# A hybrid attention block: the first weight tiles asked for earlier, the small vectors later

## The chip, the cores and the metric

The kernel runs on one core of one Trainium2 chip. The metric is the time of one execution on the device in microseconds (us). The engines are named as in the profile: PE (TensorE, the matrix products), PEld (its weight loads), DVE (VectorE), ACT (ScalarE), POOL (GpSimd) and SP (SyncE, which here only issues DMAs). SP, ACT and POOL each issue DMAs on a queue of their own; all queues share 16 DMA engines.

## The reference, cut to what matters

One decoder layer on 256 tokens of width 2048, in float32:

```
h    = rmsnorm(x) * norm_g                     # x: 256 x 2048
proj = h @ w_in                                # q, k, v, z of 12 + 8 heads, one forget column
                                               # for each of 8 heads, q and z of 4 heads, 3 gates
A: 12 heads, dilated windows, bias by distance from rel_bias, q and k normalised (q_norm_a, k_norm_a)
B: 8 heads, causal, bias from the running sum of log_sigmoid(forget column + b_forget)
M: 4 heads of 256 into mem;  k, v = (rmsnorm(mem) * mem_norm_g) @ w_mem_kv
u_i    = (o_i * silu(z_i)) @ w_proj_i          # i = A, B, M
merged = sum_i sigmoid(gate_i + b_gate_i) * u_i
out    = x + merged @ w_out
```

Nearly all of the time goes into the products with w_in, w_mem_kv, w_proj and w_out, whose 214 MB are each read once.

## The kernel before, in words

**Products.** Every float32 product is made of three: each operand is split into a high part of reduced precision and the rest (`hi`, `lo`), and PE adds hi*hi, hi*lo and lo*hi (L1337, L1338, L1339, in `passes`). A weight chunk of 2048 x 512 is cut into 16 k-tiles of 128 x 512. Two k-tiles make a *unit*: 2 k-tiles x 2 halves of the tokens x 3 passes = 12 matmuls of 512 columns. A load brings four k-tiles (1 MB) into one of four slots of `raw`. For each unit ACT writes `whi` (`hi`, L552), DVE subtracts and writes `wlo` (`lo`, L872), and PE multiplies (`unit`). `whi` and `wlo` have four slots, so ACT and DVE can be a few units ahead of PE. Eight units (`CU`) make a chunk, four chunks (q, k, v, z of four heads) make a *body* of 32 units; the bodies run one after the other, and after them the merge and the output projection.

**Order.** Each engine has one list of instructions, written out by hand. The work beside the products hangs on the unit number `s`: `beside_first(s)`, `beside_second(s)` and the constants `U_...` say at which unit an engine takes which extra step. In ACT's body the order at each `s` is: the turned tokens' high part (first chunk only), `hi` of unit `s`, the step of `beside_first(s)`, and then, at `s` = 10 and 11, `square` (L651): the squares of the first chunk's result for the q norm, scaled with `rsx`. `rsx` is 1/sqrt of the mean square of x: DVE adds up the mean (`msx`, at `s` = 8), Pool raises it to the power -0.5 (L509, signal `rootx`), and ACT's `square` of the first chunk waits for `rootx`.

**Start.** x is loaded in five pieces (columns 0 to 256, 256 to 512, and three of 512). PE turns them, so that the width lies on the partitions (`tokens_T`, L1429), ACT scales the turned piece with norm_g (`gx`) and writes the high part, DVE the low part. The first two pieces are turned ahead of the first product, the others at units 1, 3 and 5. Each turned pair of k-tiles raises the signal `xT` by one. `keep_clock(n)` issues n transposes whose result nobody reads (L1436). norm_g and mem_norm_g are loaded as 16 rows of 128 and turned by PE (L1441, L1442). For unit 0 the two k-tiles come as two loads of 256 KB, called tile 0 and tile 1 here.

**Pool's list.** Two memsets, nine DMAs of small vectors (six norm gains at L502, rel_bias, onehot, b_forget), then L509, then for each norm one small power. The gains are read as single words, one word or two for each partition; the source and the partition order give runs of 4 bytes. The program is built with `dynamic_dma_scratch_size=1024`.

Of the kernel before, what the change touches and what calls it, by code (L numbers as in the profile page):

```python
# [37 lines left out]
P = 128  # L38
D = 2048
S = 256  # L40
TT = S // P
KT = D // P
CW = 512
# [13 lines left out]
UK = 2  # L57
# [39 lines left out]
U_MERGEDT = 4  # L97
U_MERGED_SPLIT = (13, 14)
U_MEM_TURN = (8, 11, 14, 17)
U_MEM_SPLIT = (20, 21, 24, 25, 26, 27, 30, 31)  # L100
# [22 lines left out]
def hybrid_block(nc, x, mem, norm_g, mem_norm_g, w_in, b_forget, b_gate, rel_bias,  # L123
# [37 lines left out]

    gx_rows, gm_rows = part(0, P)[0:KT], part(P, P)[0:KT]
    x_sb = part(2 * D, 2 * D).rearrange("p (t d) -> p t d", t=TT)
# [8 lines left out]
    waste = part(3 * D, D)  # L172
    fbT = part(7936, S)[0:2 * B_HEADS]
    cT = part(7936, S)[0:B_HEADS]

# [66 lines left out]
    first_tile_in, first_half_in = [sem(f"first_tile_in{i}") for i in range(UK)], sem("first_half_in")  # L242
    g_in, mem_in = sem("g_in"), [sem(f"mem_in{i}") for i in range(2)]
    ident_in, cst_in = sem("ident_in"), sem("cst_in")
# [52 lines left out]
    with block as block:  # L297
# [3 lines left out]
        def _(sp):  # L301
# [13 lines left out]
            def loads(chunks, u0, before, beside=None):  # L315

                i = 0
                for view, col, tiles in chunks:
                    for k in range(0, tiles, LK):  # L320
                        slot = i % RING
                        if i >= RING:

                            sp.wait_ge(lo_done, u0 + 2 * (i - RING) + 2)
                        elif before is not None:
                            sp.wait_ge(lo_done, u0 + 2 * (last_use(slot, before) - before) + 2)
                        if before is None and i == 0:

                            for j in range(UK):
                                sp.dma_start(raw[:, 0, j], view[:, j, bass.ds(col, CW)]).then_inc(first_tile_in[j], 16)  # L330
                                if j == 0:
                                    sp_x(1)
                            sp.dma_start(raw[:, 0, UK:], view[:, UK:LK, bass.ds(col, CW)]).then_inc(load_in[0], 16)
                            sp_x(2)
                        elif before is None and i == 1:

                            sp.dma_start(raw[:, 1, 0:UK], view[:, k:k + UK, bass.ds(col, CW)])\
                              .then_inc(first_half_in, 16)
                            sp.dma_start(raw[:, 1, UK:], view[:, k + UK:k + LK, bass.ds(col, CW)])\
                              .then_inc(load_in[1], 16)  # L340
                            sp_x(3)
                        else:
                            load(view, col, k, slot)
                        if before is None and i == 2:
                            sp_x(4)
                        if before is None and i == 3:
                            sp.wait_ge(pre["gx"], 1)
                            mem_half(0)
                        if before is None and i == 5:
                            mem_half(1)  # L350
                            sp.dma_start(cst[:, P:], consts[:, P:]).then_inc(cst_in, 16)
                        if beside is not None:
                            beside(i)
                        i += 1
# [139 lines left out]
        def _(pool):  # L494
            pool.memset(half[:], -0.5).then_inc(pre["half"], 1)
            pool.wait_ge(pre["half"], 1)
            pool.memset(rel[32:33, :], 1.0).then_inc(pre["rel"], 1)
            with nc.allow_non_contiguous_dma(reason="vectors of a few hundred words, once"):
                for i, (g, w) in enumerate(((q_norm_a, 1), (k_norm_a, 1), (q_norm_b, 1), (k_norm_b, 1),
                                            (q_norm_m, 2), (k_norm_m, 2))):  # L500
                    col = i if w == 1 else 4 + 2 * (i - 4)
                    pool.dma_start(gains[:, col:col + w], g.rearrange("l (h p) -> p (l h)", p=P))\  # L502
                       .then_inc(small_in, 16)
            pool.dma_start(rel[0:32, :], rel_bias).then_inc(small_in, 16)
            pool.dma_start(oh[:], onehot).then_inc(small_in, 16)
            pool.dma_start(bf[:], b_forget.to_broadcast([P, B_HEADS])).then_inc(small_in, 16)
# [25 lines left out]
        def _(act):  # L532
# [23 lines left out]
            act.dma_start(x_sb[:, :, x_cols(0)], x_v[:, :, x_cols(0)]).then_inc(x_in[0], 16)  # L556
            act.dma_start(gm_rows, mem_norm_g.rearrange("l (k p) -> (l k) p", p=P)).then_inc(g_in, 16)

# [14 lines left out]
            def beside_first(s):  # L573
# [6 lines left out]
                if s in U_MEM_SQ:  # L580
# [3 lines left out]
                    for i in range(2):  # L584
                        act.wait_ge(mem_in[i], 16)
                    act.activation(waste, mem_sb[:, t], ACT.Square, accum_out=ssx[:, 2 + t:3 + t])\
                       .then_inc(pre["summ"], 1)
                if s == 1:

                    with nc.allow_non_contiguous_dma(reason="eight columns, once"):  # L590
                        act.dma_start(wf[:], w_in_v[:, :, F0:F0 + B_HEADS]).then_inc(wf_in, 16)
                if s in U_MEM_SPLIT:
                    n = U_MEM_SPLIT.index(s)
                    c = n // 2
                    act.wait_ge(pre["gx"], 1)
                    act.wait_ge(pre[f"mem_back{c}"], 16)
# [5 lines left out]
                    o.then_inc(pre["mT_hi"], 1)  # L602
                if s == 9:
                    act.wait_ge(wf_in, 16)
                    act.activation(wf_hi, wf[:], ACT.Copy).then_inc(pre["wf_hi"], 1)
                if s == 17:
                    act.wait_ge(pre["vneg"], 1)
                    act.activation(ls[3][:], ls[2][:], ACT.Exp).then_inc(pre["e"], 1)
                if s == 11:
# [3 lines left out]
                    act.dma_start(rel_dram, dvec).then_inc(pre["dvec_out"], 16)  # L613
                if s == 19:
                    act.wait_ge(pre["u"], 1)
                    act.activation(ls[5][:], ls[4][:], ACT.Ln).then_inc(pre["ln"], 1)
                if s in U_GATHER:
                    if s == U_GATHER[0]:
                        act.wait_ge(pre["dvec_out"], 16)
                    gather_bias(0, U_GATHER.index(s))  # L620
                if s == 25:
                    act.wait_ge(pre["crow_sb"], 1)
# [119 lines left out]
            def body(kind, g, b, lc, attn):  # L742

                u0 = g * BODY_U
                for s in range(BODY_U):
# [27 lines left out]
                    if kind == "ab" and s == U_BIAS:  # L773

                        act.wait_ge(turn_out, 64 * (2 * g + 2))
                        if fixed(b, 0):
                            act.wait_ge(pre["crow_out"], 16)
                            act.wait_ge(bias_out, 16 * 2)
# [82 lines left out]
        def _(dve):  # L861
# [72 lines left out]
            def logits(kind, a, step):  # L934
# [5 lines left out]
                if fixed(a, 0):  # L940
                    dve.wait_ge(bias_in, 16)
                    dve.wait_ge(pre["mT_hi"], 8)
                else:
                    dve.wait_ge(bias_in, 16 * (a - M_GROUPS) + 16)
# [138 lines left out]
            def beside_first(s):  # L1083
# [4 lines left out]
                if s == 8:  # L1088
# [6 lines left out]

                    dve.wait_ge(small_in, 16 * 9)
                    for i in range(AB_GROUPS):
# [9 lines left out]
                if s == 13:  # L1107
                    dve.wait_ge(pre["rootx"], 1)
                    dve.tensor_scalar(hrx[:], rsx[:, 0:2], 0.5, None, ALU.mult).then_inc(pre["halfx"], 1)
                if s == 9:  # L1110
                    dve.wait_ge(pre["wf_hi"], 1)
# [3 lines left out]
                if s in U_MEM_SPLIT:  # L1115
# [9 lines left out]
                    o.then_inc(pre["mT_lo"], 1)  # L1125
                if s == 14:
                    dve.wait_ge(pre["fbT"], 1)
                    dve.tensor_copy(fbT, side[0][0:2 * B_HEADS, 0:S]).then_inc(pre["fbT_sb"], 1)
                if s == 16:

# [11 lines left out]
                    dve.tensor_tensor(ls[2][:], ls[0][:], ls[1][:], ALU.min).then_inc(pre["vneg"], 1)  # L1142
                if s == 18:
                    dve.wait_ge(pre["e"], 1)
                    dve.tensor_scalar(ls[4][:], ls[3][:], 1.0, None, ALU.add).then_inc(pre["u"], 1)
                if s == 20:

# [8 lines left out]
                    dve.tensor_copy(ls[3][:], ls[7][:]).then_inc(pre["lf"], 1)  # L1156
                if s == 23:
                    dve.wait_ge(pre["ccol"], 1)
# [13 lines left out]
            def body(kind, g, attn, b=None):  # L1172
                u0 = g * BODY_U
                for s in range(BODY_U):
# [3 lines left out]
                    lo(u0, s)  # L1178
                    if s == 9 and kind == "ab":

# [36 lines left out]
            dve.wait_ge(pre["gxT"], 1)  # L1217
            dve.tensor_copy(gx[:], acc[0][1][:, 0:KT])
            dve.tensor_copy(gm[:], acc[0][1][:, KT:2 * KT]).then_inc(pre["gx"], 1)
            body("ab", 0, None, 0)  # L1220
# [111 lines left out]
        def _(pe):  # L1332
# [106 lines left out]
            keep_clock(4)  # L1439
            pe.wait_ge(g_in, 32)  # L1440
            pe.transpose(acc[0][1][:, 0:KT], gx_rows, ident[0:KT, 0:KT])  # L1441
            pe.transpose(acc[0][1][:, KT:2 * KT], gm_rows, ident[0:KT, 0:KT]).then_inc(pre["gxT"], 1)  # L1442
            keep_clock(4)
            tokens_T(0)
            keep_clock(6)
            tokens_T(1)
            keep_clock(6)

            def beside_first(s):
                if s in U_X:  # L1450
                    tokens_T(U_X.index(s))
                if s == 12:

# [8 lines left out]
                if s == 9:  # L1462

                    pe.wait_ge(pre["x_lo"], KT)
                    pe.wait_ge(small_in, 16 * 9)
                    pe.wait_ge(pre["rel"], 1)
                    pe.matmul(side[2][0:A_HEADS, 0:SEG], rel[:], oh[:], start=True, stop=True)\
                      .then_inc(pre["dvec"], 1)
                if s == 15:
                    pe.wait_ge(pre["fbT_sb"], 1)  # L1470
# [4 lines left out]
                    pe.wait_ge(pre["dvec_sb"], 1)  # L1475
                if s == 22:
                    pe.wait_ge(cst_in, 16)
# [114 lines left out]
```

## Time and profile before

| | |
|---|---|
| median of 3 runs | 1172.72 us (1172.53 to 1173.83) |
| the profiled execution's own time | 1174.71 us |
| its span, first to last instruction | 1172.9 us |
| PE busy | 1165.2 us, 99% of the span |
| DVE, ACT, POOL busy | 732.4, 546.6, 46.0 us |
| DMA | 275.85 MB, mean 235 GB/s |

The profiled execution is one run. Its span leaves out 1.8 us around the program that its own time has, and the profiled run lies 2.0 us above the median of the timed runs. So a difference is worked out inside the profile and then put on the median.

### The profile page before, as it was taken

The page shows a single profiled execution, that of the slowest core. Times are in us where ns is not written, and L with a number is a line of the kernel's source. Part 1 is how long each engine was busy: PE and PEld are TensorE (multiplying, and loading weights), DVE is VectorE, ACT ScalarE, POOL GpSimd, SP SyncE. Part 2 cuts the span into 40 slices and gives each one's busy share as a digit, 9 for nine tenths or more (in the row PEclk, how much of TensorE's full clock was granted, in tenths as well). Part 3 has the DMA queues.
Part 4 walks back from the last instruction along what each step waited for, and adds up shares of the span by engine and source line. Part 5 has one row for each costly group of instructions (what it writes and reads, how often), then busy time and mean ns, then how long its engine had stood idle before and what let it go on. Part 6 is the DMA issues. An engine that isn't in the chain of part 4 may idle for free.

```text
span 1172.9 us, 14512 instructions
## 1 busy us (share of the span) xinstructions
PE 1165.2 (99%) x5312; PEld 968.2 (83%) x5312; DVE 732.4 (62%) x905; ACT 546.6 (47%) x670; POOL 46.0 (4%) x36
## 2 busy tenths in 40 slices
PE   8999999999999999999999999999999999999998
PEld 7788888888888888888888888888888888888887
DVE  4877588576567567567566565665556556555653
ACT  4666445445445545535545444434434443443432
POOL 2111000000010000000000000000000000000000
PEclk9999999999999999999999999999999999999999
DMA  9988789658577578677677796567548546765861
GB/s 309 329 261 318 234 267 328 225 188 287 192 235 271 195 261 282 199 257 242 237 245 222 258 274 207 173 215 261 198 148 299 189 157 224 255 205 199 283 244 37
DMA packets 147613, 275.85 MB, mean 235 GB/s; under 512 B 9393, under 2 KB 32613, under 8 KB 147568
## 3 DMA queue, kind: packets, MB, share of 16 engines
q1 hardware_dynamic: 135632, 258.57, 66.0%
q10 hardware_dynamic: 11488, 16.62, 4.5%
q8 instruction: 28, 0.46, 0.2%
q0 software_dynamic: 448, 0.06, 0.1%
q14 instruction: 17, 0.14, 0.0%
HBM read 251.34 MB, written 26.24 MB: 237 GB/s over the span
## 4 chain that ended last, share of the span: by engine, by line
PE 99%; DMA 1%; SPq 0%; DVE 0%; issue 0%
PE acc L1337 32%; PE acc L1339 32%; PE acc L1338 32%; PE side L1381 1%; DMA group<-in_x_dram 1%; PE side L1373 0%; PE side L1397 0%; PE side L1406 0%; PE side L1408 0%; PE side L1404 0%; PE side L1382 0%; PE side L1429 0%; PE side L1457 0%; PE side L1459 0%; PE acc L1436 0%; PE acc L1429 0%
## 5 line engine op out<-in xcount | busy, mean ns | idle before, releaser
L872 DVE TENSOR_TENSOR w_lo<-w_raw,w_hi 128x1024 fp32r<-128x1024 f32 x407 | 496.1, 1222 | 371.5 <-ACT w_hi L552 370.8
L552 ACT ACTIVATE w_hi<-w_raw 128x1024 fp32r<-128x1024 f32 x407 | 430.0, 1060 | 540.4 <-PE acc L1339 530.7
L1337 PE MATMUL acc<-w_hi,hT_hi 128*128 128x512 f32 x1152 | 450.7, 391 | 0.1
L1338 PE MATMUL acc<-w_lo,hT_hi 128*128 128x512 f32 x1152 | 448.6, 389 | 0.0
L1339 PE MATMUL acc<-w_hi,hT_lo 128*128 128x512 f32 x1152 | 448.6, 389 | 0.0
L1337 PEld LDWEIGHTS acc<-w_hi,hT_hi 128*128 128x128 f32 x1152 | 216.6, 188 | 46.8 <-DVE w_lo L872 1.3
L1339 PEld LDWEIGHTS acc<-w_hi,hT_lo 128*128 128x128 f32 x1152 | 216.5, 188 | 45.3
L1338 PEld LDWEIGHTS acc<-w_lo,hT_hi 128*128 128x128 f32 x1152 | 216.6, 188 | 44.1
L1337 PE MATMUL acc<-w_hi,mT_hi 128*128 128x512 f32 x256 | 99.8, 390 | 0.0
L1338 PE MATMUL acc<-w_lo,mT_hi 128*128 128x512 f32 x256 | 99.6, 389 | 0.0
L1339 PE MATMUL acc<-w_hi,mT_lo 128*128 128x512 f32 x256 | 99.6, 389 | 0.0
L1339 PE MATMUL acc<-w_hi,ozT_lo 128*128 128x512 f32 x224 | 87.2, 389 | 0.0
L1337 PE MATMUL acc<-w_hi,ozT_hi 128*128 128x512 f32 x224 | 87.1, 389 | 0.0
L1338 PE MATMUL acc<-w_lo,ozT_hi 128*128 128x512 f32 x224 | 87.1, 389 | 0.0
L1337 PEld LDWEIGHTS acc<-w_hi,mT_hi 128*128 128x128 f32 x256 | 48.1, 188 | 10.2 <-issue 0.2
L1338 PEld LDWEIGHTS acc<-w_lo,mT_hi 128*128 128x128 f32 x256 | 48.1, 188 | 9.9
L1339 PEld LDWEIGHTS acc<-w_hi,mT_lo 128*128 128x128 f32 x256 | 48.1, 188 | 9.9
L1337 PEld LDWEIGHTS acc<-w_hi,ozT_hi 128*128 128x128 f32 x224 | 42.1, 188 | 8.7
L1338 PEld LDWEIGHTS acc<-w_lo,ozT_hi 128*128 128x128 f32 x224 | 42.0, 188 | 8.7
L1339 PEld LDWEIGHTS acc<-w_hi,ozT_lo 128*128 128x128 f32 x224 | 42.0, 188 | 8.7
L528 POOL TENSOR_TENSOR rs<-ms,half 128x8 f32<-128x8 f32 x8 | 20.5, 2562 | 353.4 <-DVE ms L900 353.4
L651 ACT ACTIVATE group<-acc,rsx 128x512 f32<-128x512 f32 x28 | 19.2, 686 | 21.9 <-PE acc L1339 21.2
(177 smaller groups left out, 578.6 us busy)
## 6 DMA issues: line engine op xcount, KB each, us to landing
w_raw<-in_w_in_dram SPq DMA_DIRECT2D x142, 1024.0 KB, 6.4
w_raw<-in_w_mem_kv_dram SPq DMA_DIRECT2D x16, 1024.0 KB, 6.4
w_raw<-in_w_out_dram SPq DMA_DIRECT2D x16, 1024.0 KB, 5.2
w_raw<-in_w_proj_a_dram SPq DMA_DIRECT2D x12, 1024.0 KB, 5.1
w_raw<-in_w_proj_m_dram SPq DMA_DIRECT2D x8, 1024.0 KB, 5.0
w_raw<-in_w_proj_b_dram SPq DMA_DIRECT2D x8, 1024.0 KB, 5.0
turned_oz<-group SPq DMA_DIRECT2D x44, 128.0 KB, 4.7
group<-turned_oz SPq DMA_DIRECT2D x11, 512.0 KB, 4.5
```

Source lines behind the costliest of these rows:

```text
L528: pool.tensor_tensor(rs[:], ms[:], half[:], ALU.pow).then_inc(roots, 1)
L552: act.activation(whi[:, s % RING], raw[:, slot, UK * (s % 2):UK * (s % 2) + UK], ACT.Copy)\
L651: act.activation(qn[:, t], acc[w][t][:], ACT.Square, scale=rsx[:, r:r + 1]).then_inc(squares, 1)
L872: dve.tensor_tensor(wlo[:, s % RING], raw[:, (s // 2) % RING, UK * (s % 2):UK * (s % 2) + UK], whi[:, s % RING].bitcast(F32), ALU.subtract ...
L1337: pe.matmul(banks[t][:], hi, whi[:, s % RING, j], start=first and j == 0, stop=False)
L1338: pe.matmul(banks[t][:], hi, wlo[:, s % RING, j], start=False, stop=False)
L1339: return pe.matmul(banks[t][:], lo, whi[:, s % RING, j], start=False, stop=last and j == UK - 1)
L1381: pe.matmul(side[h][:, 0:S], q2[x][:, h], k2[y][:, :, h], start=n == 0, stop=n == 2)
```

## The change

- Tile 0 is asked for on ACT's queue, right behind x's first piece, where mem_norm_g stood. On SP's queue tile 1 comes first and x's second piece after it.
- mem_norm_g is no longer loaded as rows and turned by PE with norm_g. Pool loads it straight into `gm`, in four pieces of 128 partitions x 4 single words, signal `gm_in`.
- Pool waits until six pairs of x are turned (`xT` at 6) before it asks for any small vector. rel_bias and onehot come first and have a signal of their own (`rel_in`), then the six gains, the four pieces of mem_norm_g, and b_forget.
- Four `keep_clock` transposes ahead of x's first piece go; behind the first piece there are nine for six, behind the second two for six.
- The forget column's weights (wf) are asked for at unit 4 instead of 1, and the steps that hang on them come three units later on every engine. DVE's step with the gains moves from unit 8 to 12, and its copy of the gain from unit 9 to 13.
- The tiles fbT and cT move within `group`; DVE's first logits wait for `crow_out` instead of ACT's load of the bias.

```diff
+U_GAINS = 12
-    gx_rows, gm_rows = part(0, P)[0:KT], part(P, P)[0:KT]
+    gx_rows = part(0, P)[0:KT]
-    fbT = part(7936, S)[0:2 * B_HEADS]
-    cT = part(7936, S)[0:B_HEADS]
+    fbT = part(6144, S)[0:2 * B_HEADS]
+    cT = part(6144 + S, S)[0:B_HEADS]
...
-                            for j in range(UK):
-                                sp.dma_start(raw[:, 0, j], view[:, j, bass.ds(col, CW)]).then_inc(first_tile_in[j], 16)
-                                if j == 0:
-                                    sp_x(1)
+                            sp.dma_start(raw[:, 0, 1], view[:, 1, bass.ds(col, CW)]).then_inc(first_tile_in[1], 16)
+                            sp_x(1)
...
             pool.memset(rel[32:33, :], 1.0).then_inc(pre["rel"], 1)
+            pool.wait_ge(pre["xT"], 6)
+            pool.dma_start(rel[0:32, :], rel_bias).then_inc(rel_in, 16)
+            pool.dma_start(oh[:], onehot).then_inc(rel_in, 16)
...
                     pool.dma_start(gains[:, col:col + w], g.rearrange("l (h p) -> p (l h)", p=P))\
                        .then_inc(small_in, 16)
-            pool.dma_start(rel[0:32, :], rel_bias).then_inc(small_in, 16)
-            pool.dma_start(oh[:], onehot).then_inc(small_in, 16)
+                for k in range(0, KT, 4):
+                    pool.dma_start(gm[:, k:k + 4], mem_norm_g.rearrange("l (k p) -> p (l k)", p=P)[:, k:k + 4])\
+                       .then_inc(gm_in, 16)
             pool.dma_start(bf[:], b_forget.to_broadcast([P, B_HEADS])).then_inc(small_in, 16)
             pool.wait_ge(pre["rel"], 1)
             pool.wait_ge(pre["meanx"], 1)
...
-            act.dma_start(gm_rows, mem_norm_g.rearrange("l (k p) -> (l k) p", p=P)).then_inc(g_in, 16)
+            view, col = body_chunks("a", 0)[0]
+            act.dma_start(raw[:, 0, 0], view[:, 0, col:col + CW]).then_inc(first_tile_in[0], 16)
-                if s == 1:
+                if s == 4:
                         act.dma_start(wf[:], w_in_v[:, :, F0:F0 + B_HEADS]).then_inc(wf_in, 16)
-                    act.wait_ge(pre["gx"], 1)
+                    act.wait_ge(gm_in, 64)
                     act.wait_ge(pre[f"mem_back{c}"], 16)
...
-                            act.wait_ge(pre["crow_out"], 16)
...
+                    dve.wait_ge(pre["crow_out"], 16)
...
-                    dve.wait_ge(small_in, 16 * 9)
+                if s == U_GAINS:
+                    dve.wait_ge(small_in, 16 * 7)
...
-                    if s == 9 and kind == "ab":
+                    if s == (U_GAINS + 1 if fixed(g, 0) else 9) and kind == "ab":
...
-            dve.tensor_copy(gm[:], acc[0][1][:, KT:2 * KT]).then_inc(pre["gx"], 1)
+            dve.tensor_copy(gx[:], acc[0][1][:, 0:KT]).then_inc(pre["gx"], 1)
...
             keep_clock(4)
-            pe.wait_ge(g_in, 32)
-            pe.transpose(acc[0][1][:, 0:KT], gx_rows, ident[0:KT, 0:KT])
-            pe.transpose(acc[0][1][:, KT:2 * KT], gm_rows, ident[0:KT, 0:KT]).then_inc(pre["gxT"], 1)
-            keep_clock(4)
+            pe.wait_ge(g_in, 16)
+            pe.transpose(acc[0][1][:, 0:KT], gx_rows, ident[0:KT, 0:KT]).then_inc(pre["gxT"], 1)
             tokens_T(0)
-            keep_clock(6)
+            keep_clock(9)
             tokens_T(1)
-            keep_clock(6)
+            keep_clock(2)
...
-                    pe.wait_ge(small_in, 16 * 9)
+                    pe.wait_ge(rel_in, 16 * 2)
```

The steps on the forget column that come three units later are not repeated here: on PE 12 to 15, 15 to 18 and 22 to 25; on DVE 9 to 12, 14 to 17, 16 to 19, 18 to 21, 20 to 23 and 23 to 26; on ACT 9 to 12, 17 to 20, 19 to 22 and 25 to 28.

## Rows read from the trace of the kernel before

**Rows 1.** The page: busy time by engine, and the chain's shares by engine.
```profile
PE 1165.2 (99%) x5312; PEld 968.2 (83%) x5312; DVE 732.4 (62%) x905; ACT 546.6 (47%) x670; POOL 46.0 (4%) x36
...
PE 99%; DMA 1%; SPq 0%; DVE 0%; issue 0%
```

**Rows 2.** The timeline of the start: us, duration, instruction, idle time before it.
```profile
2.13 0.45 SPq L313 DMA_DIRECT2D group<-in_x_dram  x1
2.62 0.47 SPq L330 DMA_DIRECT2D w_raw<-in_w_in_dram  x1
...
8.70 1.11 PE L1429 MATMUL side<-cst,group 128*128 128x128 f32 x4 [0.83 <-DMA group<-in_x_dram]
9.21 0.63 ACT L541 ACTIVATE w_hi<-w_raw 128x512 fp32r<-128x512 f32 x1 [1.17 <-DMA w_raw<-in_w_in_dram]
...
9.60 1.49 PE L1436 MATMUL acc<-cst 128*128 128x128 f32 x6
...
10.74 0.78 PE L1337 MATMUL acc<-w_hi,hT_hi 128*128 128x512 f32 x1
...
12.17 0.63 PE L1337 MATMUL acc<-w_hi,hT_hi 128*128 128x512 f32 x1
...
12.60 0.50 PE L1338 MATMUL acc<-w_lo,hT_hi 128*128 128x512 f32 x1
...
12.93 0.39 PE L1339 MATMUL acc<-w_hi,hT_lo 128*128 128x512 f32 x1
...
13.16 0.39 PE L1337 MATMUL acc<-w_hi,hT_hi 128*128 128x512 f32 x1
```

**Rows 3.** DMA issues: line, count, KB each, us from issue to landing.
```profile
wf<-in_w_in_dram ACTq DMA_DIRECT2D x1, 64.0 KB, 18.9
mem_means<-msx POOLq DMA_DIRECT2D x4, 0.2 KB, 7.6
...
group<-in_norm_g_dram SPq DMA_DIRECT2D x1, 8.0 KB, 2.3
...
gains<-in_q_norm_a_dram POOLq DMA_DIRECT2D x1, 0.5 KB, 4.3
...
gains<-in_q_norm_m_dram POOLq DMA_DIRECT2D x1, 1.0 KB, 7.9
gains<-in_k_norm_m_dram POOLq DMA_DIRECT2D x1, 1.0 KB, 5.2
```

**Rows 4.** The timeline of Pool alone, to the first power.
```profile
1.33 0.74 POOL L502 DMA_DIRECT2D gains<-in_q_norm_a_dram  x1 [0.33 <-issue]
...
3.14 0.56 POOL L502 DMA_DIRECT2D gains<-in_k_norm_b_dram  x1
3.67 0.76 POOL L502 DMA_DIRECT2D gains<-in_q_norm_m_dram  x1
11.91 0.74 POOL L502 DMA_DIRECT2D gains<-in_k_norm_m_dram  x1 [7.49 <-issue]
...
13.72 0.57 POOL L506 DMA_DIRECT2D bf<-in_b_forget_dram  x1
36.05 0.74 POOL L509 TENSOR_TENSOR rsx<-msx,half 128x2 f32<-128x2 f32 x1 [21.76 <-DVE msx L1093]
```

**Rows 5.** The timeline of ACT alone, around its first squares.
```profile
37.41 0.69 ACT L651 ACTIVATE group<-acc,rsx 128x512 f32<-128x512 f32 x1 [1.15 <-PE acc L1339]
38.00 1.05 ACT L552 ACTIVATE w_hi<-w_raw 128x1024 fp32r<-128x1024 f32 x1
...
42.64 1.05 ACT L552 ACTIVATE w_hi<-w_raw 128x1024 fp32r<-128x1024 f32 x1
```

**Rows 6.** The timeline of PE alone: the turned x at unit 3, unit 11's first product.
```profile
21.18 1.04 PE L1429 MATMUL acc<-cst,group 128*128 128x128 f32 x8
...
46.34 0.39 PE L1337 MATMUL acc<-w_hi,hT_hi 128*128 128x512 f32 x1
```

**Rows 7.** The page's costliest groups: busy us, mean ns of one, idle before.
```profile
L872 DVE TENSOR_TENSOR w_lo<-w_raw,w_hi 128x1024 fp32r<-128x1024 f32 x407 | 496.1, 1222 | 371.5 <-ACT w_hi L552 370.8
```

More of the change, by code:

```diff
@@ L242, in hybrid_block @@
     first_tile_in, first_half_in = [sem(f"first_tile_in{i}") for i in range(UK)], sem("first_half_in")
-    g_in, mem_in = sem("g_in"), [sem(f"mem_in{i}") for i in range(2)]
+    g_in, gm_in, rel_in, mem_in = sem("g_in"), sem("gm_in"), sem("rel_in"), [sem(f"mem_in{i}") for i in range(2)]
     ident_in, cst_in = sem("ident_in"), sem("cst_in")
@@ L602, in beside_first @@
                     o.then_inc(pre["mT_hi"], 1)
-                if s == 9:
+                if s == 12:
                     act.wait_ge(wf_in, 16)
                     act.activation(wf_hi, wf[:], ACT.Copy).then_inc(pre["wf_hi"], 1)
-                if s == 17:
+                if s == 20:
                     act.wait_ge(pre["vneg"], 1)
@@ L613, in beside_first @@
                     act.dma_start(rel_dram, dvec).then_inc(pre["dvec_out"], 16)
-                if s == 19:
+                if s == 22:
                     act.wait_ge(pre["u"], 1)
@@ L620, in beside_first @@
                     gather_bias(0, U_GATHER.index(s))
-                if s == 25:
+                if s == 28:
                     act.wait_ge(pre["crow_sb"], 1)
@@ L1109, in beside_first @@
                     dve.tensor_scalar(hrx[:], rsx[:, 0:2], 0.5, None, ALU.mult).then_inc(pre["halfx"], 1)
-                if s == 9:
+                if s == 12:
                     dve.wait_ge(pre["wf_hi"], 1)
@@ L1125, in beside_first @@
                     o.then_inc(pre["mT_lo"], 1)
-                if s == 14:
+                if s == 17:
                     dve.wait_ge(pre["fbT"], 1)
                     dve.tensor_copy(fbT, side[0][0:2 * B_HEADS, 0:S]).then_inc(pre["fbT_sb"], 1)
-                if s == 16:
+                if s == 19:
                     dve.wait_ge(pre["fb"], 1)
@@ L1142, in beside_first @@
                     dve.tensor_tensor(ls[2][:], ls[0][:], ls[1][:], ALU.min).then_inc(pre["vneg"], 1)
-                if s == 18:
+                if s == 21:
                     dve.wait_ge(pre["e"], 1)
                     dve.tensor_scalar(ls[4][:], ls[3][:], 1.0, None, ALU.add).then_inc(pre["u"], 1)
-                if s == 20:
+                if s == 23:
                     dve.wait_ge(pre["ln"], 1)
@@ L1156, in beside_first @@
                     dve.tensor_copy(ls[3][:], ls[7][:]).then_inc(pre["lf"], 1)
-                if s == 23:
+                if s == 26:
                     dve.wait_ge(pre["ccol"], 1)
@@ L1217, in _ @@
             dve.wait_ge(pre["gxT"], 1)
-            dve.tensor_copy(gx[:], acc[0][1][:, 0:KT])
-            dve.tensor_copy(gm[:], acc[0][1][:, KT:2 * KT]).then_inc(pre["gx"], 1)
+            dve.tensor_copy(gx[:], acc[0][1][:, 0:KT]).then_inc(pre["gx"], 1)
             body("ab", 0, None, 0)
@@ L1451, in beside_first @@
                     tokens_T(U_X.index(s))
-                if s == 12:
+                if s == 15:
                     pe.wait_ge(pre["x_lo"], KT)
@@ L1468, in beside_first @@
                       .then_inc(pre["dvec"], 1)
-                if s == 15:
+                if s == 18:
                     pe.wait_ge(pre["fbT_sb"], 1)
@@ L1475, in beside_first @@
                     pe.wait_ge(pre["dvec_sb"], 1)
-                if s == 22:
+                if s == 25:
                     pe.wait_ge(cst_in, 16)
```

## The prediction

> **What bounds the kernel now.** I read the page first, then the timeline of the first 50 us engine by engine, then the landings of the DMAs, and last who waits for whom. The page shows one limit: PE is busy for 1165.2 of 1172.9 us, and the chain that ended last is 99% PE [rows 1]. So a moment in which PE has no product to start is lost for good, since nothing later has slack in which to win it back; and work on ACT, DVE or Pool costs something only if PE ends up waiting for it. The reader is to see two places. The first is the start: PE waits for x's second piece until 8.70, turns it, spends 1.49 us on six dummy transposes, and starts its first product at 10.74; products come 0.43 us apart until 12.9 and 0.23 us apart after that, as 512 columns do at 1.2 and at 2.4 GHz [rows 2]. The second is unit 11, whose first product starts at 46.34 [rows 6]: PE has run without a gap up to there, and what has to be ready for it passes through ACT, which at 37.41 takes the first square (L651) with a factor that Pool worked out at 36.05 (L509) [rows 4, 5]. Today Pool's queue is empty by then: its last DMA was issued at 13.72, and it stood idle for 21.76 us before that small operation [rows 4].
>
> **The change part by part. The start.** Tile 0 of the weights moves to ACT's queue in place of mem_norm_g, tile 1 moves ahead of x's second piece, and Pool's nine DMAs leave the start. Tile 1 and the x piece then trade places: today the x piece sets PE going at 8.70 and tile 1 sets ACT going at 9.21, with issues 0.49 us apart [rows 2]. I take the x piece at 8.7 as before, because one transfer more is ahead of it and the small ones are gone; the bounds are half a microsecond earlier and one later. Behind its transposes two dummies stand in place of six. At 1.49 us for six, that is some 0.9 us with the overlap of their ends, so the first product starts near 9.9. If the spacing still falls at 12.9, two products more are done by then, worth 0.23 us each: **0.4 us gained**. The transposition of mem_norm_g and the other dummies that go or come ahead of the x piece cost nothing, because PE waits for that piece; without that wait (0.83 us) nine dummies for six would cost 0.6. Bounds: 0.9 us gained if the faster spacing comes as much earlier, 0.3 us lost if the x piece comes one microsecond later. The three units by which the forget-gate steps and wf move cost nothing: they hang on wf, which took 18.9 us to land [rows 3]; asked for at unit 4, near 23, it lands near 42 for a step that ACT reaches behind its w_hi of unit 12, which starts at 42.64 [rows 5]. The wait for crow_out moves from ACT at unit 28 to DVE a body later, behind everything it waits for. If these covers were gone, each would cost the part of its own wait that exceeds PE's lead of one to two units (2.7 us each).
>
> **Pool's queue.** This is the part that I expect to decide. All of Pool's DMAs now stand behind a wait for the sixth turned pair of x, and four new ones join them: mem_norm_g in pieces of 128 x 4 single words. Behind all of them in Pool's order stands L509, and ACT waits for that. So I follow Pool's clock.
>
> The eight transposes that hold the sixth pair start at 21.18 and take 1.04 us [rows 6]; 0.4 us earlier, Pool starts at 21.8. A DMA of Pool takes it 0.56 us for 128 single words and 0.76 us for 256 [rows 4]. rel, oh and four vectors take 6 x 0.56 = 3.34 us, so q_norm_m is issued at 25.14.
>
> Now the sixth vector. In the trace Pool issued five (4 x 128 and 256 words: 768) and then stood still for 7.49 us, to 11.91, with "issue" as the only reason [rows 4]. The fifth had been issued at 3.67 and took 7.9 us to land, which is 11.57 [rows 3, 4]: Pool went on 0.34 us after the landing. I read this as a limit on single words in flight, at least 768 and below the 1,024 that the sixth would have made. Two pieces of mem_norm_g are 1,024 words, so by the same rows no two of them can be in flight: the second, third and fourth each wait for the one before to land. And rel, oh and the first five vectors make some 833 pieces (32 and 33 rows, and 768 words), so that k_norm_m waits for q_norm_m as it does now. That is four waits for a landing. 
> One landing, from issue: 5.2 us for 256 words among running loads (k_norm_m), 7.9 us for 256 words behind four others (q_norm_m), 7.6 us for mem_means, and 4.3 us at the least (q_norm_a) [rows 3]. I take 6.0 for all four, nearest to k_norm_m because the loads run then too, and more than it because 512 words are twice as many. No row has 512 single words; the bounds are 4.3 and 7.9.
>
> So k_norm_m is issued at 25.14 + 6.0 + 0.34 = 31.48, the first piece at 32.22, the second at 38.56, the third at 44.90, the fourth at 51.24. The fourth takes 1.16 us to issue (0.20 more for each 128 words), b_forget 0.57: **Pool is free at 53.0**, or 28.97 + 4 landings. Then L509 0.74, ACT's square 0.59 to the next instruction, the w_hi behind it 1.05 [rows 4, 5], its w_lo 1.22 [rows 7] and 0.1 of handing on: unit 11 starts at 56.7. Without the wait it would start at 46.34 - 0.4 = 45.94. **PE stands still for 10.8 us.**
>
> Behind ACT's stopped square are queued w_hi of unit 11 and all later ones, two squares of mem and the rel copy; DVE's w_lo waits for ACT, and PE for DVE. DVE's own wait for the vectors at unit 12 ends with b_forget's landing near 58 and comes no later than its turn.
>
> **After the stall.** PE idled before 8.70 and then its products came 0.43 us apart until it had been busy to 12.9, 4.2 us on [rows 2]. If that recurs, some ten products cost 0.20 us more each: **2.0 us**, and they cover the squares that ACT catches up on meanwhile. Bounds: nothing if the clock stays at 2.4 GHz and ACT keeps up, 3.6 us if both cost.
>
> **The sum**, on the profiled execution: span 1172.9 - 0.4 + 10.8 + 2.0 = 1185.3 us, 12.4 more. Its own time was 1174.71 (1.8 around the span) and the median of the three runs 1172.72, so the median should be **1185.1 us**.
>
> **Rivals.** *Single words are slower still.* The five landings (from 1.33 + 4.3 to 3.67 + 7.9) show the last one 2.5 us behind the fourth. If 512 words take 2.5 us more than k_norm_m's 256, each piece takes 7.7, and q_norm_m 7.9 as before: Pool is free at 60.0, PE stands for 17.8 us, and the time is near 1192. The longer landing of mem_means speaks for it, k_norm_m's 5.2 against.
>
> *Landings are short, and nothing is lost.* This ends on the other side. PE isn't stopped if Pool is free by 42.2, that is, if the four landings take 3.3 us each or less. norm_g on SP's queue landed in 2.3 [rows 3]; with that Pool is free at 38.2, unit 11 isn't held, and only the 0.4 us remain: 1172.3. Against it, all the DMAs of Pool shown took 4.3 us and more. The Trainium skill (DMA: Bandwidth & Descriptors, Anatomy of one DMA — SWDGE (gpsimd) path) has about 2.0 us and the bytes at 436 GB/s for a DMA from Pool, which is this rival; the trace's 5.2 us for 1 KB is against it here.
>
> *The limit is one of five DMAs, not of words, or there is none.* Five at a time makes two waits: the fifth is issued at 24.0 and lands at 30.0, the tenth at 33.6 and 39.6, and the last three are out near 43. Unit 11 then starts at 46.7, 0.8 late, and the time is 1173.1. With no limit Pool is through at 32 and the time is 1172.3. The halt after exactly five allows the count as well; the trace holds no case that parts it from the words.
>
> **How the numbers follow.** The stall by four landings near 6 us: 0.66. The slower words: 0.19. Short landings: 0.05. A limit by count or none: 0.09. A start that gains over 0.2% (2.3 us, about what a measurement of this kernel can tell from no change): 0.01, because all products before 12.9 at double speed give less. So slower 0.85, same 0.14, faster 0.01. Landings of 4.3 us give a stall of 4.0 us and, with no loss after it, 1176.3; landings of 7.9 with the larger loss after it give 1194.3. The range is 1177 to 1194; it leaves out the 0.14 at 1172 to 1173 and a little above.
>
> **What would show it.** Right: Pool's timeline has four halts after q_norm_m and between the pieces of mem_norm_g, L509 starts near 53, ACT's first square is put down to Pool, and PE has one gap of 9 to 18 us before unit 11. The start shows the first product near 9.9. Wrong: L509 stays near 36, or it comes late and ACT's square does not wait; or the halts are there but each is under 3.3 us. A further gap of PE at units 15 to 25 would mean that the moved forget-gate steps are not covered.

## The result and the profile after

The changed kernel takes 1180.99 us (median of 4 executions, 1180.44 to 1181.64) against 1173.24 for the one before: 7.75 us more, ratio 1.0064 with a 95% interval of 1.0052 to 1.0076. It is slower, as forecast, by 62% of the 12.4 us that were forecast, and inside the range.

The page after: busy time by engine, the chain's shares, and one of the costliest groups (busy, mean ns | idle before, releaser). They answer to [rows 1, 7].

```profile
PE 1164.5 (99%) x5306; PEld 966.9 (82%) x5306; DVE 732.0 (62%) x904; ACT 545.6 (46%) x670; POOL 48.0 (4%) x40
...
PE 97%; issue 2%; POOL 1%; DMA 0%; DVE 0%; ACT 0%; POOLq 0%; ACTq 0%
...
L1341 PE MATMUL acc<-w_hi,hT_hi 128*128 128x512 f32 x1152 | 451.4, 392 | 7.4 <-DVE w_lo L875 7.4
```

PE is as busy as before; what is new is Pool in the chain, and one idle stretch of 7.4 us ahead of a product that waited for DVE's `w_lo`. It is the only gap of PE behind the start. Pool's timeline after shows where it comes from; it answers to [rows 4].

```profile
18.96 0.71 POOL L498 DMA_DIRECT2D rel<-in_rel_bias_dram  x1 [17.97 <-PE acc L1433]
...
22.36 0.74 POOL L504 DMA_DIRECT2D gains<-in_q_norm_m_dram  x1
28.73 0.74 POOL L504 DMA_DIRECT2D gains<-in_k_norm_m_dram  x1 [5.63 <-issue]
29.46 0.77 POOL L507 DMA_DIRECT2D gm<-in_mem_norm_g_dram  x1
35.65 0.76 POOL L507 DMA_DIRECT2D gm<-in_mem_norm_g_dram  x1 [5.42 <-issue]
41.40 0.75 POOL L507 DMA_DIRECT2D gm<-in_mem_norm_g_dram  x1 [5.00 <-issue]
45.13 0.76 POOL L507 DMA_DIRECT2D gm<-in_mem_norm_g_dram  x1 [2.98 <-issue]
45.87 0.55 POOL L509 DMA_DIRECT2D bf<-in_b_forget_dram  x1
46.55 0.72 POOL L512 TENSOR_TENSOR rsx<-msx,half 128x2 f32<-128x2 f32 x1
```

Seven DMAs go out in a row, then Pool halts four times with "issue" as the only reason, at the four places that were forecast. Its power (L509 before, L512 here) starts at 46.55 in place of 36.05. ACT's timeline follows, with one line of DVE's; it answers to [rows 5].

```profile
47.37 0.69 ACT L655 ACTIVATE group<-acc,rsx 128x512 f32<-128x512 f32 x1 [14.87 <-POOL rsx L512]
47.95 1.05 ACT L555 ACTIVATE w_hi<-w_raw 128x1024 fp32r<-128x1024 f32 x1
48.90 1.90 ACT L590 ACTIVATE group<-group 128x2048 f32<-128x2048 f32 x1
...
52.55 1.05 ACT L555 ACTIVATE w_hi<-w_raw 128x1024 fp32r<-128x1024 f32 x1
...
54.02 1.22 DVE L875 TENSOR_TENSOR w_lo<-w_raw,w_hi 128x1024 fp32r<-128x1024 f32 x1
```

ACT stands for 14.87 us and names Pool. The `w_hi` at 47.95 is unit 11's, the one at 52.55 unit 12's; between them lie the square of mem, the rel copy and the second square that had queued up. DVE's line is unit 12's `w_lo`, which ends at 55.24. PE's timeline, which answers to [rows 2, 6]:

```profile
7.52 0.60 PE L1433 MATMUL side<-cst,group 128*128 128x128 f32 x4
...
8.09 0.48 PE L1341 MATMUL acc<-w_hi,hT_hi 128*128 128x512 f32 x1
...
42.56 0.39 PE L1343 MATMUL acc<-w_hi,hT_lo 128*128 128x512 f32 x1
50.31 0.80 PE L1341 MATMUL acc<-w_hi,hT_hi 128*128 128x512 f32 x1 [7.36 <-DVE w_lo L875]
50.90 0.63 PE L1342 MATMUL acc<-w_lo,hT_hi 128*128 128x512 f32 x1
51.33 0.63 PE L1343 MATMUL acc<-w_hi,hT_lo 128*128 128x512 f32 x1
...
55.31 0.48 PE L1341 MATMUL acc<-w_hi,hT_hi 128*128 128x512 f32 x1
```

x's second piece is turned at 7.52 and the first product starts at 8.09, in place of 8.70 and 10.74. The last product of unit 10 starts at 42.56, so unit 11 was due some 0.23 us later, at 42.8. From the power's start at 46.55 to unit 11 at 50.31 it is 3.76 us. Unit 11 then lasts to 55.31, 5.0 us in place of 2.7, with most of its products 0.43 us apart. The stretches around it, in a view of busy time by engine with the granted clock (third column from the right) and DMA share and GB/s:

```profile
30.00:43.00 13.00, 12.95 (x55) 9.60 (x53) 5.74 (x10) 2.50 (x3) 1.73 (x3) 1.00 1.07 358
43.00:50.00 7.00, 0.00 (x0) 0.00 (x0) 0.97 (x1) 2.63 (x3) 2.01 (x3) 0.87 0.12 12
50.00:55.00 5.00, 4.69 (x11) 3.73 (x12) 3.75 (x6) 4.29 (x6) 0.81 (x1) 0.50 0.50 118
```

In the gap PE does nothing, and the loads stop too (12 GB/s): SP waits 15.5 us for DVE's turning of mem (L1083), which stands behind the same `w_lo` in DVE's list. The granted clock is at half in the stretch after it, the 1.2 GHz level.

### The profile page after: what moved, and what is told of

Read it like the earlier page. It is cut to its first block, busy times and chain, and to the rows that moved or that the text cites. A ratio compares the mean times of both kernels' runs of the same rounds, so it can differ in the third digit from the quotient of the medians.

```text
span 1179.2 us, 14504 instructions
## 1 busy us (share of the span) xinstructions
PE 1164.5 (99%) x5306; PEld 966.9 (82%) x5306; DVE 732.0 (62%) x904; ACT 545.6 (46%) x670; POOL 48.0 (4%) x40
## 4 chain that ended last, share of the span: by engine, by line
PE 97%; issue 2%; POOL 1%; DMA 0%; DVE 0%; ACT 0%; POOLq 0%; ACTq 0%
PE acc L1341 31%; PE acc L1343 31%; PE acc L1342 31%; PE side L1385 1%; PE side L1377 0%; PE side L1401 0%; PE side L1410 0%; PE side L1412 0%; PE side L1408 0%; PE side L1386 0%; POOL gains L504 0%; DMA cst<-in_consts_dram 0%; PE acc L1440 0%; POOL gm L507 0%; PE side L1433 0%
```

## The experiments

The theory: thirteen DMAs stand ahead of Pool's power, and the room for their single words makes Pool halt for landings. The main rivals: the moved forget-gate steps cost the time; the single words cost by their presence, wherever they stand; the limit is a count of DMAs. Medians of before beside these runs were 1172.9 to 1173.2.

**Pool's part alone.** The kernel before, with only Pool's list (and what reads it) from the change; tiles, dummies and steps as before.

```diff
+            pool.wait_ge(pre["xT"], 6)
+            pool.dma_start(rel[0:32, :], rel_bias).then_inc(rel_in, 16)
+            pool.dma_start(oh[:], onehot).then_inc(rel_in, 16)
...
+                for k in range(0, KT, 4):
+                    pool.dma_start(gm[:, k:k + 4], mem_norm_g.rearrange("l (k p) -> p (l k)", p=P)[:, k:k + 4])\
+                       .then_inc(gm_in, 16)
```

> The kernel before with Pool's part of the change alone: Pool waits for the sixth turned pair of x, then asks for rel_bias, onehot, the gains, mem_norm_g in four pieces and b_forget, all ahead of its first power; the order of the first tiles, the dummies and the forget-gate steps are those of the kernel before. If Pool's order alone is the loss, PE stands still ahead of unit 11 for 6 to 8 us and the time is 1180 to 1182. If the loss needs the earlier start, which brings ACT to its square sooner, the gap is shorter by as much: 1178 to 1180. If other parts cause it: 1173.

1181.99 us, ratio 1.0069 (1.0053 to 1.0084). The timelines of Pool, ACT and PE, one line each:

```profile
47.56 0.72 POOL L514 TENSOR_TENSOR rsx<-msx,half 128x2 f32<-128x2 f32 x1
48.37 0.69 ACT L655 ACTIVATE group<-acc,rsx 128x512 f32<-128x512 f32 x1 [14.34 <-POOL rsx L514]
51.31 0.79 PE L1341 MATMUL acc<-w_hi,hT_hi 128*128 128x512 f32 x1 [7.04 <-DVE w_lo L875]
```

The power is late, ACT names Pool, and PE stands for 7.0 us ahead of unit 11. The other parts are not needed for the loss.

**The same DMAs behind the power.** The changed kernel, mem_norm_g's pieces moved behind the first norm's power.

```diff
                 pool.tensor_tensor(rs[:, 0:n], ms[:, 0:n], half[:, 0:n], ALU.pow).then_inc(roots, 1)
+                if i == 0:
...
+                        for k in range(0, KT, 4):
+                            pool.dma_start(gm[:, k:k + 4], mem_norm_g.rearrange("l (k p) -> p (l k)", p=P)[:, k:k + 4])\
+                               .then_inc(gm_in, 16)
```

> The changed kernel with the four pieces of mem_norm_g still on Pool, but asked for behind the power and behind the first norm's power. The same DMAs with the same halts, now with nothing behind them that anyone waits for. If it is the place in Pool's order that costs, the power starts near 32.5, three halts of 3 to 6 us show up later, PE has no gap, 1169.5 to 1170.5 us. If these single-word DMAs cost by their presence (contention with the loads), part of the loss stays: 1173 or more. If the moved steps are the cause: 1179 to 1181.

1172.48 us, ratio 1.0000 (0.9990 to 1.0010): 8.5 us less than the changed kernel. Pool's timeline:

```profile
33.88 0.72 POOL L509 TENSOR_TENSOR rsx<-msx,half 128x2 f32<-128x2 f32 x1 [2.51 <-DVE msx L1099]
44.39 2.54 POOL L513 TENSOR_TENSOR rs<-ms,half 128x8 f32<-128x8 f32 x1 [9.79 <-DVE ms L905]
46.90 0.81 POOL L517 DMA_DIRECT2D gm<-in_mem_norm_g_dram  x1
53.24 0.76 POOL L517 DMA_DIRECT2D gm<-in_mem_norm_g_dram  x1 [5.54 <-issue]
```

The power waits for DVE again, the halts are still there, and PE has no gap. So it is the place in Pool's order, not the words or the moved steps. The time did not fall to the 1170 that was expected; the second profile of the kernel before, below, says why.

**Twice the room.** The changed kernel with one number changed.

```diff
-    nc = _bacc.Bacc("TRN2", ..., dynamic_dma_scratch_size=1024)
+    nc = _bacc.Bacc("TRN2", ..., dynamic_dma_scratch_size=2048)
```

> The changed kernel with one number changed: 2048 bytes reserved for Pool's descriptors in place of 1024. If the halts come from the room for descriptors, nine DMAs go out without a halt, the second piece of mem_norm_g waits for the vectors to land near 28, at most one more halt follows, Pool is free by 30 to 34, PE is not stopped, 1169.5 to 1171 us. If they come from a count of DMAs, or from each such DMA waiting for the one before it whatever the room, the four halts stay and so does the time, 1180 to 1181.

1173.15 us, ratio 1.0001 (0.9991 to 1.0011). Pool's timeline:

```profile
25.03 0.77 POOL L507 DMA_DIRECT2D gm<-in_mem_norm_g_dram  x1
30.26 1.50 POOL L507 DMA_DIRECT2D gm<-in_mem_norm_g_dram  x2 [4.46 <-issue]
36.93 0.75 POOL L507 DMA_DIRECT2D gm<-in_mem_norm_g_dram  x1 [5.17 <-issue]
37.67 0.55 POOL L509 DMA_DIRECT2D bf<-in_b_forget_dram  x1
38.35 0.72 POOL L512 TENSOR_TENSOR rsx<-msx,half 128x2 f32<-128x2 f32 x1
```

Nine DMAs go out before the first halt, and there are two halts in place of four. The room sets the halts, then, not a fixed count and not each DMA by itself. The power still starts at 38.35, later than the 30 to 34 expected, and ACT waits 5.4 us for Pool; PE waits only 0.2 us, ahead of unit 12. As with the last kernel, the time did not come down to what was expected, 1169.5 to 1171 here.

**The kernel before once more**, for a second profile.

> The kernel before, unchanged, for a second profile. The profiled execution of before took 1174.7 us and its granted clock rose to 2.4 GHz at 12.8 us; the timed ones took 1172.3 to 1173.9. If the moment of the rise varies from execution to execution, this one rises near 10 to 11, its first products come 0.23 us apart sooner, its span is near 1171, and most of the 3.5 us that the changed kernel was ahead at unit 8 was the difference between two executions and no gain of the change. If the rise stays at 12.8 and the span near 1172.9, the gain of the start was real and something later in the mended kernel gives it back.

1172.57 us, span 1170.8. PE's timeline:

```profile
7.56 0.66 PE L1429 MATMUL side<-cst,group 128*128 128x128 f32 x4 [0.20 <-DMA group<-in_x_dram]
8.06 0.82 PE L1436 MATMUL acc<-cst 128*128 128x128 f32 x6
8.63 0.48 PE L1337 MATMUL acc<-w_hi,hT_hi 128*128 128x512 f32 x1
8.95 0.39 PE L1338 MATMUL acc<-w_lo,hT_hi 128*128 128x512 f32 x1
...
12.16 1.09 PE L1429 MATMUL side<-cst,group 128*128 128x128 f32 x8 [0.53 <-DMA group<-in_x_dram]
13.34 0.50 PE L1337 MATMUL acc<-w_hi,hT_hi 128*128 128x512 f32 x1
```

The same program has its first product at 8.63, not 10.74, at 0.23 us spacing from the start; unit 8 starts at 35.0 in place of 37.2. The trace's record of the full clock begins at 6.7 us here and at 12.8 in the execution of [rows 2], some 6 us later; x's second piece, too, is turned at 7.56 and not at 8.70. Of the 3.5 us that the changed kernel was ahead at unit 8 (33.7), 2.2 were the difference between two executions of the same program. The other 1.3 are not shown to be a gain: the kernel with the pieces behind the power has the changed kernel's start and begins unit 8 at 35.05.

**The start alone**: the kernel before with the new order of tiles and dummies; the vectors at the start, the steps where they were, mem_norm_g's pieces behind the first norm's power.

```diff
+                            sp.dma_start(raw[:, 0, 1], view[:, 1, bass.ds(col, CW)]).then_inc(first_tile_in[1], 16)
+                            sp_x(1)
...
-            keep_clock(6)
+            keep_clock(9)
             tokens_T(1)
-            keep_clock(6)
+            keep_clock(2)
```

> The kernel before with the order of the first tiles and the numbers of dummies of the changed one, and with mem_norm_g on Pool behind the first norm's power; vectors at the start, steps where they were. If the start is what the change gains by, 1172.3 to 1172.7, some 0.4 us under the kernel before; if the gain needed the vectors out of the way, 1173.

1173.89 us, ratio 1.0003 (0.9994 to 1.0012): no gain from the order. PE's timeline shows why:

```profile
12.40 1.09 PE L1434 MATMUL side<-cst,group 128*128 128x128 f32 x8 [1.03 <-DMA group<-in_x_dram]
```

The first product starts at 8.37, 0.26 us sooner than in the second profile of the kernel before. But x's third piece, which unit 1 needs, lands no sooner: PE waits 1.03 us for it in place of 0.53, and turns it at 12.40 in place of 12.16. With the vectors behind it, PE turns it in the changed kernel at 10.95, without a wait.

**The steps back**: the kernel with the pieces behind the power, with wf and the forget-gate steps at their old units. It differs from the one just told by Pool's wait for x alone.

```diff
-                if s == 4:
+                if s == 1:
                         act.dma_start(wf[:], w_in_v[:, :, F0:F0 + B_HEADS]).then_inc(wf_in, 16)
...
```

> The mended kernel (mem_norm_g's pieces behind the first norm's power) with wf and the forget-gate steps back at the units of the kernel before. If moving them by three units costs nothing, the time stays at 1172.5 (1171.9 to 1173.1). If the moved steps took from what the start gives, this one is 1 to 2 us faster than 1172.5; if they give something, it is slower.

1172.47 us against 1172.48 with the steps moved: moving them costs and gives nothing that can be measured. Against the start alone it is 1.4 us less, though the two intervals (0.9983 to 1.0001 here) overlap a little; the last pair below shows it more clearly. What the change gains at all comes from the vectors that wait.

**The vectors at the start, Pool's wait for x removed** from the changed kernel.

```diff
-            pool.wait_ge(pre["xT"], 6)
```

> The changed kernel without Pool's wait for the sixth turned pair of x, so that its thirteen DMAs start near 1 us. The halts stay, four of about 5 us, and Pool is free near 29, ahead of the mean: no gap of PE. But the single words are back among the first transfers. If they were what made x's second piece late, the first product comes later than 8.1 and the time lies between 1170 and 1173; if the order of the tiles alone made the start faster, the first product stays near 8.1 and the time is 1169.5 to 1170.5. If the loss comes from the moved steps: 1179 to 1181.

1174.26 us, ratio 1.0015 (1.0005 to 1.0024), outside every range expected. The halts were 5.3 to 7.1 us, longer than expected, so Pool's power started at 34.98, not 29. The first product came at 8.9. The waits of ACT, DVE and PE:

```profile
36.17 0.69 ACT L654 ACTIVATE group<-acc,rsx 128x512 f32<-128x512 f32 x1 [1.23 <-POOL rsx L511]
44.62 1.30 DVE L1082 STREAM_TRANSPOSE group<-group 128x512 f32<-128x512 f32 x2 [5.55 <-DMA turned_mem<-group]
48.41 0.50 PE L1340 MATMUL acc<-w_hi,hT_hi 128*128 128x512 f32 x1 [1.96 <-DVE w_lo L874]
```

ACT waits 1.2 us for Pool, and unit 11 starts at 43.57 without a wait: the stall goes when Pool starts early enough, as the theory has it. PE's gap of 2.0 us comes later, ahead of unit 12, and is not Pool's power. Unit 12's `w_hi` was done at 42.4; its `w_lo` came late because DVE had first waited 5.55 us for the transfer of mem's turned rows out to memory. Why that transfer took so long here is not shown, and the profiled execution lies 1.6 us above the median, so the gap need not be in every one.

**mem_norm_g from ACT's queue**, in one DMA behind wf.

```diff
+                        act.dma_start(gm[:], mem_norm_g.rearrange("l (k p) -> p (l k)", p=P)).then_inc(gm_in, 16)
```

> The changed kernel with the four pieces of mem_norm_g taken off Pool and loaded in one DMA from ACT's queue at unit 4. If the halts between these pieces hold Pool's power (and through it ACT's first square and PE), three of four halts go, Pool is free near 30, ahead of the mean it needs (near 32.5), PE has no gap, and the time is that of the kernel before less the 3.5 us that the changed one is ahead at unit 8: 1169.5 to 1170.5 us. If the loss comes from the forget-gate steps moved by three units, or from DVE's later step with the gains, the gap stays and the time is 1179 to 1181.

1178.60 us, a miss. Pool did as expected (free at 30.3, the power waits for DVE), but ACT had a new stall:

```profile
19.38 8.20 ACTq L593 DMA_DIRECT2D gm<-in_mem_norm_g_dram  x1
...
27.68 0.84 ACT L566 ACTIVATE hT_hi<-acc,gx 128x256 fp32r<-128x256 f32 x2 [6.14 <-issue]
```

Issuing 2,048 single words behind the 2,048 runs of wf kept ACT's own list for 8.20 us; PE stood for 5.1 us and its clock fell. The words had been moved from one engine's way into another's.

**The clock kept up through the gap**: the changed kernel with 60 dummies ahead of unit 11.

```diff
...
+                if s == 11:
+                    keep_clock(60, side[3])
```

> The changed kernel with 60 dummy transposes (some 6.4 us) on PE just ahead of unit 11, so that PE is busy through its gap of 7.4 us. The gap itself stays, since ACT still waits for Pool. If the lower clock after the gap costs 2.0 us, the products of unit 11 come 0.23 us apart and the time falls from 1181.0 to 1179.0 (1178.5 to 1179.5). If the lower clock was covered by ACT's catching up, the products are faster but unit 12 waits as much longer, and the time stays at 1180.5 to 1181.5.

1182.07 us, ratio 1.0071 (1.0056 to 1.0086): no gain. PE's timeline:

```profile
43.20 6.71 PE L1440 MATMUL side<-cst 128*128 128x128 f32 x60
50.06 0.50 PE L1341 MATMUL acc<-w_hi,hT_hi 128*128 128x512 f32 x1
50.40 0.40 PE L1342 MATMUL acc<-w_lo,hT_hi 128*128 128x512 f32 x1
...
55.05 0.50 PE L1341 MATMUL acc<-w_hi,hT_hi 128*128 128x512 f32 x1 [1.93 <-DVE w_lo L875]
...
56.42 0.63 PE L1342 MATMUL acc<-w_lo,hT_hi 128*128 128x512 f32 x1
56.85 0.63 PE L1343 MATMUL acc<-w_hi,hT_lo 128*128 128x512 f32 x1
```

Unit 11 ran at 2.4 GHz, and unit 12 started at 55.05 all the same, because its `w_hi` was queued behind ACT's squares. So the 2.3 us after the gap in the changed kernel are ACT's and DVE's: there, too, unit 12 starts (55.31) right behind its `w_lo` (55.24), and the lower clock of unit 11 hides in that wait. The dummies did not keep the clock up for good. After this second stop it fell, and unit 12 has its products 0.43 us apart, with a mean granted clock of 0.66 from 55 to 60; it lasts 4.4 us in place of 2.7. That is why this kernel is no faster, and in the profiles 1.4 us slower.

**Dummies ahead of the identity**, on the kernel with the pieces behind the power; then with the steps back as well; then without Pool's wait for x.

```diff
+            dve.memset(part(1024, P), 0.0).then_inc(pre["warm"], 1)
...
+            pe.wait_ge(pre["warm"], 1)
+            for _ in range(6):
+                pe.matmul(acc[0][0][:, 0:P], part(1024, P), part(1024, P), start=True, stop=True)
```

> The mended kernel (mem_norm_g's pieces behind the first norm's power) with six dummy products of a cleared tile on PE at the very start, ahead of the wait for the identity, so that PE is busy from about 1 us in place of 3.7. If the start is paced by the moment at which the clock rises (9.9 in the mended kernel's profile), the rise comes 2 to 3 us earlier, ahead of the first product, and the time falls by about 1 us, to 1171 to 1172. If x's second piece paces the start, the first product stays near 8.1 to 9 and the time at 1172.5.

> The mended kernel with both the early dummies and the forget-gate steps back at the units of the kernel before. Alone, the dummies gave 1171.8 and the steps 1172.5 against 1172.5 for the mended kernel and 1173.0 for the one before. If the two add up, 1171.0 to 1171.8; the dummies' profile lost 0.7 us again between unit 8 and unit 32, at a load that ACT waited for 2.5 us, and if that load is the bound now, the time stays at 1171.8 with or without the steps.

> The kernel with the early dummies and the steps back, and without Pool's wait for x: the nine vectors go out at the start, as in the kernel before, and only mem_norm_g's pieces come later. If the vectors' single words among the first transfers delay the tiles and x, the first product comes 0.5 us later or more and the time is 0.5 to 1 us above the one with the wait. If they delay nothing, both times are the same within 0.3 us, and putting them off gains nothing.

1171.79 (ratio 0.9991, 0.9982 to 1.0000), **1171.75 (0.9985, 0.9976 to 0.9994)** and 1173.44 (0.9996, 0.9987 to 1.0005). The first two are the fastest kernels here and don't differ, so the steps add nothing to the dummies; the second is 1.4 us under the kernel before in its own comparison and 9.2 under the changed one. The dummies themselves give 0.7 us, with intervals that overlap. The last two differ by the wait for x alone, 1.7 us, and the slowest execution of the one with the wait (1172.63) is under the fastest of the other (1172.71). Their first ten microseconds, the one with the wait first, in the view by stretches:

```profile
0.00:10.00 10.00, 8.51 (x45) 7.30 (x46) 3.33 (x8) 5.18 (x9) 0.39 (x6) 1.00 0.77 251
```

```profile
0.00:10.00 10.00, 8.95 (x44) 7.82 (x45) 3.30 (x8) 4.18 (x8) 4.51 (x13) 1.00 0.67 216
```

With Pool's vectors among them the DMA engines move 216 GB/s, without them 251; unit 1 starts at 13.4 against 11.5.

## Why the prediction was right, and where its sizes were off

**Pool's queue, shown.** The four halts, the power behind them, ACT's square, unit 11: each step came at its place, Pool's part alone gave the whole loss, and moving the pieces behind the power took it away. From the power to unit 11 the prediction had 3.7 us; it was 3.76.
**The term that was mis-sized: 6.0 us for each landing.** q_norm_m took 5.96 (28.32 less 22.36), and the three pieces that were waited for 5.85, 5.45 and 3.43: 20.7 us in all in place of 24.0, and the stall 7.5 (50.31 less unit 11's due time of 42.8) in place of 10.8. The 3.3 us are the same 3.3. The first three landings were near the estimate. The last of the four was short because the stall had by then stopped the loads: 12 GB/s in the stretch from 43 to 50. Where the loads went on, with the same pieces behind the power, Pool's halts between them were 5.3 to 5.8 us throughout. One duration was taken for four landings, though the wait itself changes the traffic that made them long. The Trainium skill (DMA: Bandwidth & Descriptors, Anatomy of one DMA — SWDGE (gpsimd) path) has some 2.0 us for a DMA from Pool; the trace comes near it (2.5 us, the last piece) only once the loads have stopped.

Smaller errors: a piece of 512 words takes Pool 0.76 us to issue, as one of 256 does, not 1.16, and 6 x 0.56 is 3.36, not 3.34. That Pool started at 18.96 and not at 21.8 changed next to nothing, since unit 11 was due 3.1 us earlier too.

**After the stall, 2.0 us.** The term came to 2.3, but for a cause that stood only beside it. The slower products were as described, but what sets unit 12 is the backlog of ACT and DVE: with unit 11 at the full clock it started only 0.3 us sooner.

**The start, 0.4 us gained.** The median agrees: 0.4 us between before (1172.86) and the kernel with the pieces behind the power (1172.48), inside the noise. That is luck, for the way was wrong. x's second piece was turned at 7.52 and not at 8.7, and the first product came at 8.09 and not at 9.9; but the kernel before has 7.56 and 8.63 in its second profile. The order of the tiles gives nothing measurable. The vectors out of the first ten microseconds give 1.4 to 1.7 us, by way of x's third piece; the prediction had them only as a balance for one transfer more ahead of the second. And it was read from an execution whose clock rose late, which a single profile cannot show.

**The sum of the terms.** In the profiles 3.5 us gained, 7.5 of stall and 2.3 behind it make 6.3 more, as the spans do (1179.2 less 1172.9). The medians differ by 7.75 because the profiled execution of before lay 1.5 us above its median.

**The steps by three units** cost nothing, as forecast, and PE has no gap at units 15 to 25. **The rivals**: short landings and a limit by count are both excluded by the halts after seven DMAs and by their lengths; the slower words as well, for 512 words landed no later than 256.

## What to carry to other kernels

A DMA that scatters single words is priced by what is queued behind its issue. Where the issuing engine's list holds a small operation that others wait for, such DMAs belong behind it. And a stall that feeds on transfers should not be priced with the busy machine's latency throughout, since it stops the traffic that makes it long.

Before a gain of a few microseconds at a kernel's start is read from two profiles, take a second profile of the same program: here two executions differed by 2.2 us.

## What the hardware showed unasked

The issue of one DMA of 2,048 single words, behind another of 2,048 short runs, held ACT's list for 8.20 us; wf's own issue took 0.39. Pool's issue of 512 words took 0.76.

The granted clock fell while PE stood still: the mean is 0.87 of full over the idle stretch, then 0.50 over the five microseconds in which PE worked again. In the kernel with the 60 dummies a stop of 1.93 us was followed by such a fall as well.
